# Order of low halves, loads and products in the three pairs of each feed-forward stage

## The reference, cut to what matters

```python
D_MODEL, SEQ, D_FF = 1024, 256, 2816

def swiglu(h, w_in, w_out):                       # first block, stage FFN0
    gate, up = jnp.split(h @ w_in, 2, axis=-1)
    return (jax.nn.silu(gate) * up) @ w_out

def _swiglu(x, wg, wu, wd):                       # stages FFN1 to FFN4
    return (jax.nn.silu(x @ wg) * (x @ wu)) @ wd

def second_block(x, norm_g, ffn_w_gate, ffn_w_up, ffn_w_down, ...):
    for l in range(2):
        g = norm_g[l]
        h = _swiglu(_rmsnorm(x, g[0]), ffn_w_gate[l, 0], ffn_w_up[l, 0], ffn_w_down[l, 0])
        x = x + 0.5 * _rmsnorm(h, g[1])
        h = _rmsnorm(x, g[2])
        h = _mixer_even(h, ...) if l % 2 == 0 else _mixer_odd(h, ...)
        x = x + _rmsnorm(h, g[3])
        h = _swiglu(_rmsnorm(x, g[4]), ffn_w_gate[l, 1], ffn_w_up[l, 1], ffn_w_down[l, 1])
        x = x + 0.5 * _rmsnorm(h, g[5])
    return x
```

## Time and profile before

| | us |
|---|---|
| three runs: median (lowest to highest) | 1301.72 (1301.05 to 1302.33) |
| profiled execution, its time | 1308.35 |
| its span from first to last instruction | 1306.6 |
| PE busy | 1268.1 |
| DVE busy | 970.9 |
| ACT busy | 744.5 |
| POOL busy | 151.7 |

### The profile page before, as it was taken

How to read it: one execution, slowest core, us unless ns; L and a number is a source line. 1 busy time by engine, 2 the same in 40 slices (tenths; PEclk the granted TensorE clock), 3 DMA queues, 4 the chain that set the end, 5 groups by cost and what they waited for, 6 DMA issues and landing times. The chain is left out here.

```text
span 1306.6 us, 17142 instructions
## 1 busy us (share of the span) xinstructions
PE 1268.1 (97%) x6759; PEld 1039.4 (80%) x6759; DVE 970.9 (74%) x989; ACT 744.5 (57%) x922; POOL 151.7 (12%) x132
## 2 busy tenths in 40 slices
PE   8999999999999989999999999999899999999998
PEld 7887888887778868877878777888788897788776
DVE  4476776555898876676797877897776687898865
ACT  4433644444755655657665556565657655755653
POOL 3000197000680000100000000000000100000000
PEclk9999999999999999999999899999999999999989
DMA  9996486555568555652756645956753544668452
GB/s 335 360 401 217 173 283 207 183 184 193 164 235 257 193 145 194 199 173 88 277 192 216 188 150 161 322 198 189 192 177 130 170 143 125 218 232 258 164 149 88
DMA packets 154299, 265.51 MB, mean 203 GB/s; under 512 B 9528, under 2 KB 94836, under 8 KB 152692
## 3 DMA queue, kind: packets, MB, share of 16 engines
q1 hardware_dynamic: 149504, 243.28, 54.8%
q0 software_dynamic: 4352, 21.06, 6.7%
q10 hardware_dynamic: 372, 0.19, 0.1%
HBM read 248.73 MB, written 1.05 MB: 191 GB/s over the span
## 5 line engine op out<-in xcount | busy, mean ns | idle before, releaser
L2151 DVE TENSOR_TENSOR w_lo<-raw,w_hi 128x2048 fp32r<-128x2048 f32 x147 | 340.8, 2324 | 79.4 <-ACT w_hi L1539 79.1
L1539 ACT ACTIVATE w_hi<-raw 128x2048 fp32r<-128x2048 f32 x147 | 280.2, 1911 | 87.8 <-PE ps L763 46.7
L761 PE MATMUL ps<-w_lo,hT_hi 128*128 128x512 f32 x368 | 150.2, 408 | 21.0 <-DVE w_lo L2151 16.4
L762 PE MATMUL ps<-w_hi,hT_hi 128*128 128x512 f32 x368 | 147.6, 401 | 0.0
L763 PE MATMUL ps<-w_hi,hT_lo 128*128 128x512 f32 x368 | 147.1, 400 | 0.0
L761 PE MATMUL ps<-w_lo,xT_pair 128*128 128x512 f32 x308 | 122.4, 397 | 0.0
L763 PE MATMUL ps<-w_hi,xT_pair 128*128 128x512 f32 x308 | 120.2, 390 | 0.0
L762 PE MATMUL ps<-w_hi,xT_pair 128*128 128x512 f32 x308 | 120.0, 390 | 0.0
L761 PE MATMUL ps<-xT_pair,w_hi 128*128 128x256 f32 x368 | 108.3, 294 | 0.2 <-DVE xT_pair L2540 0.2
L761 PEld LDWEIGHTS ps<-w_lo,hT_hi 128*128 128x128 f32 x368 | 71.5, 194 | 42.4 <-issue 19.8
L762 PE MATMUL ps<-xT_pair,w_hi 128*128 128x256 f32 x368 | 104.8, 285 | 0.0
(11 more groups left out here) (335 smaller groups left out, 2663.2 us busy)
## 6 DMA issues: line engine op xcount, KB each, us to landing
raw<-in_ffn_w_down SPq DMA_DIRECT2D x88, 512.0 KB, 4.5
arena<-in_ffn_w_up SPq DMA_DIRECT2D x48, 512.0 KB, 5.4
raw<-in_ffn_w_in SPq DMA_DIRECT2D x44, 512.0 KB, 4.6
raw<-in_ffn_w_gate SPq DMA_DIRECT2D x40, 512.0 KB, 4.1
raw<-in_ffn_w_up SPq DMA_DIRECT2D x40, 512.0 KB, 5.2
raw<-in_conv_w_in SPq DMA_DIRECT2D x24, 512.0 KB, 9.4
arena<-in_ffn_w_gate SPq DMA_DIRECT2D x24, 512.0 KB, 4.6
rows<-in_ffn_w_gate SPq DMA_DIRECT2D x24, 512.0 KB, 6.5
```

The lines of the kernel that those rows point to most:

```text
L761: pe.matmul(o, a_hi, b_lo, start=first, stop=False, skip_group_check=True)
L762: pe.matmul(o, a_hi, b_hi, start=False, stop=False, skip_group_check=True)
L1539: act.activation(w_hi[:, slot_of(n), :], raw[:, raw_slot(n), :], ACT.Copy).then_inc(hi_ready, 1)
L2151: dve.tensor_tensor(w_lo[:, slot_of(n), :], source(n), w_hi[:, slot_of(n), :].bitcast(F32), ALU.subtract).then_inc(raw_done, 1)
```

## The change

It touches only `load_seven`, `row_part` and the three versions of `seven`:

- SP loads down unit 7 ahead of the first pair's blocks and of the wait for `x_new`, and block 3 (b_21) ahead of block 2 (b_22).
- PE's `row_part` takes the eight products with the high weights first, waiting for `hi_ready` alone, and then the four with the low weights, behind `raw_done`. `down` does the like for each tile of tokens: high by high, high by low weights, low hidden by high weights, with a wait ahead of each.
- DVE, first pair: `x_sums_lo` moves ahead of unit 7's low half, `hT_lo` ahead of t_1, unit 8's low half ahead of t_2. Third pair: `hT_lo` and unit 30's low half move ahead of t_1, unit 32's low half ahead of `hT_lo` of down unit 33.

No computation is added or left out.

```diff
--- before.py
+++ after.py
@@ -594,12 +594,12 @@
                 chunk(2, 1)
                 down_rows(4, 0)
                 chunk(5, 2)
+                down_rows(7, 1)
                 sp.wait_ge(x_new, x_count(s - 1, 1, 1))
                 block(0, 0)
                 block(1, 0)
-                down_rows(7, 1)
+                block(3, 0)
                 block(2, 0)
-                block(3, 0)
                 down_rows(12, 2)
                 chunk(16, 5)
                 sp.wait_ge(raw_done, n + 10)
@@ -932,11 +932,16 @@
 
             def row_part(n, h, t, banks):
 
-                hi, lo = unit(n)
+                hi, lo = w_hi[:, slot_of(n), :], w_lo[:, slot_of(n), :]
+                pe.wait_ge(hi_ready, n + 1)
                 for k in range(4):
                     c = slice(k * 512, (k + 1) * 512)
-                    mm = product(ps[:, banks[t], :], xT_hi[:, 4 * h + k, tok(t)], xT_lo[:, 4 * h + k, tok(t)], hi[:, c], lo[:, c],
-                                 h == 0 and k == 0, h == 1 and k == 3)
+                    pe.matmul(ps[:, banks[t], :], xT_hi[:, 4 * h + k, tok(t)], hi[:, c], start=h == 0 and k == 0, stop=False, skip_group_check=True)
+                    pe.matmul(ps[:, banks[t], :], xT_lo[:, 4 * h + k, tok(t)], hi[:, c], start=False, stop=False, skip_group_check=True)
+                pe.wait_ge(raw_done, n + 1)
+                for k in range(4):
+                    mm = pe.matmul(ps[:, banks[t], :], xT_hi[:, 4 * h + k, tok(t)], lo[:, k * 512:(k + 1) * 512], start=False,
+                                   stop=h == 1 and k == 3, skip_group_check=True)
                 return mm
 
             def row_first(n, banks):
@@ -986,9 +991,25 @@
 
                 def down(o, i):
 
-                    pe.wait_ge(hT_ok, NCH * f + i + 1)
+                    hi, lo = w_hi[:, slot_of(n + o), :], w_lo[:, slot_of(n + o), :]
+
+                    def products(t, aT, v, first):
+                        for k in range(2):
+                            for h in range(2):
+                                mm = pe.matmul(ps[:, 4 + 2 * t + h, :], aT[:, k, tok(t)], v[:, k * D + h * 512:k * D + (h + 1) * 512],
+                                               start=first and k == 0, stop=False, skip_group_check=True)
+                        return mm
+
+                    if i == 0:
+                        pe.wait_ge(hT_ok, NCH * f + 1)
+                    pe.wait_ge(hT_hi_ok, NCH * f + i + 1)
+                    pe.wait_ge(hi_ready, n + o + 1)
                     for t in range(TOKT):
-                        mm = down_part(n + o, hT_hi, hT_lo, 0, t, i == 0, False)
+                        products(t, hT_hi, hi, i == 0)
+                        pe.wait_ge(raw_done, n + o + 1)
+                        products(t, hT_hi, lo, False)
+                        pe.wait_ge(hT_ok, NCH * f + i + 1)
+                        mm = products(t, hT_lo, hi, False)
                     mm.then_inc(w_used, 1)
 
                 def pair(p, at, a, b, c, fill):
@@ -2445,12 +2466,12 @@
                 x_sums()
                 row_hidden(1, (2, 3))
                 lo(6)
+                x_sums_lo()
                 lo(7)
-                x_sums_lo()
+                turned(1, 2)
                 sum_first(0)
-                turned(1, 2)
+                lo(8)
                 sum_second(0)
-                lo(8)
                 sum_third(0)
                 row_hidden(2, (0, 1))
                 lo(9, 10, 11)
@@ -2484,13 +2505,13 @@
                 pair_hidden(1, 0)
                 pair_hidden(1, 1)
                 lo(29)
-                sum_first(2)
                 turned(6, 1)
                 lo(30)
+                sum_first(2)
                 sum_second(2)
-                lo(31)
+                lo(31, 32)
                 turned(7, 3)
-                lo(32, 33)
+                lo(33)
                 c_11(2, 2)
                 lo(34, 35, 36)
                 c_22(2)
```

## The result

| | before | after |
|---|---|---|
| timed on one chip, median of 5 runs each (lowest to highest) | 1302.14 (1301.05 to 1304.47) | 1273.71 (1272.33 to 1274.76) |
| ratio, with its 95% interval | | 0.9778 (0.9764 to 0.9792) |
| profiled execution | 1308.35 | 1274.00 |
| its span | 1306.6 | 1272.3 |
| mean granted clock of that execution | 0.989 | 0.998 |

The timed gain is 28.4 us, the forecast was 31.7. The two profiled executions are 34.3 us apart. All three numbers have to be explained.

A forecast was written before the change was run, and what follows sets the result against it. TensorE (PE), busy 97% of the span, was taken as the bound, losing time to waits for low halves and slow clock. Third pair 26.6 plus first pair 5.1 made 31.7 us off 1301.72: 1270.0 us, range 1265 to 1283.

The forecast's parts named there:

- Third pair, both edits: Units 30 to 33 of the four FFN stages: nearly all waiting and slow clock goes, 26.6 us saved in all.
- First pair: Units 7 to 9: unit 7 starts without a wait; 3.5 us saved in FFN1, 0.8 each in FFN2 and FFN3, together 5.1.
- Now the load is issued when unit 4's low half is done: First pair: unit 7's load no longer stands behind two blocks and the wait for x_new; part of the 5.1 us.
- Row units and added waits: Row units' new product order and some 170 more PE waits: value 0, at the upper end 3 us lost.
- the waits hang on the program, not on the profiler, so I take the same 31.7 off: Final sum: the 31.7 us read from the profile also come off the timed median of 1301.72, giving 1270.0.
- The rule weighed in the prediction: Slow clock over 740 to 753, FFN2: rule says 3.4 us lost, against 2.8 in unit 30; it would give 1267.
- K: Rival: PE's clock still falls after the remaining gaps, costing 10.7 us in all, about 1280; chance 0.08.
- D: Rival: DVE becomes the bound, a microsecond or two lost at units 31 and 33 per stage, 1275 to 1278; chance 0.07.
- S: Rival: slower; third pair's accumulating DMA T4 lands late as three megabytes meet, PE waits at unit 36, 1315; chance 0.04.
- N: Rival: no gain; the waits reappear one unit on at full size, 1300; chance 0.03.

## Why the prediction was right, and where it was not

The time, 1273.71, lies in the forecast's own range (1266 to 1276), 3.7 us above its point. The waits and their places were right in the main; the price in time of the slow clock was too high.

- *Third pair, both edits: right.* 27.3 us in the profile, 26.6 forecast. Unit 30's low half followed `hT_lo` by DVE's own lengths as worked out, and t_1, t_2 and the low halves of 31 to 33 kept up. The small waits were 0.28 and 0.28, forecast 0.26 and 0.55. The two edits alone and undone show that both are needed: without DVE's order 13.3 us come back, without the products' 5.0 (by the profiles 15.8 and 6.2).
- *First pair: the sum near, in part by luck.* 5.5 us in the profile, 5.1 forecast, with 1.23 us at unit 9 where 1.5 was forecast. But 1.0 of the 5.5 is FFN3's, a wait that some executions with the old first pair have and others do not; the forecast's 0.8 for it was read off the one that had it. The step "Now the load is issued when unit 4's low half is done" has no share in it: with the loads alone as before nothing changed. And the first pair's edits are worth 4 us only where the products are as before; with the new ones 1.4 (2.4 by the profiles). The step took the edits one by one and forgot that down unit 7 has the new products too.
- *Row units and added waits: right.* 0, by the kernel with the old rows.
- *Short waits: missed.* 1.5 us in the second pairs, at down unit 20; they are gone in each kernel with the new down products and there in each without.
- *The step that failed: "the waits hang on the program, not on the profiler, so I take the same 31.7 off".* The waits do. The slow clock behind them does not: it followed the same wait in two stages of four in one execution and in four of four in another. The profiled execution of before had 0.989 and the most frequent timed run 0.993, and 0.004 x 1300 x 0.84 is 4.4 us. Between profile and time the gain shrank by 5.9: the profile of before lies 6.2 above its median (1308.35 - 1302.14), that of after 0.3 above its own. Of the 5.9 the clock is 4.4, or 5.5 if the run with the median of 1302.14 had 0.994, as the table's 1301.8 suggests. The rest is not explained; the rounding of the clock (0.0005 x 1300 = 0.65 on either side) and the wait of FFN3 may hold it. The 31.7 had the full price of five falls in it: I knew that the profile lay 6.6 above the median and did not ask what of that was clock.
- *The rule weighed in the prediction.* The Trainium skill (TensorE: Matmul & The Clock Gate, Terms) counts the throttled time times one minus the clock's share. The line through the runs has 0.84 of that, and the unit with a window of 0.68 took 1.6 us longer, where (1 - 0.68) x 5.3 says 1.7; over the stretch in which PE partly stands idle it says more than was lost (3.4 for 2.8). So it would have made the forecast worse, by 3 us, as the prediction had it.

The rivals: *K* (the clock still falls) no, the changed kernel's clock fell in none of the four stages. The reason given against it (no fall after 1.10 us) was too weak, as one did come after 1.09 in an experiment. What is left at units 30 and 33 is 0.28, and the 1.23 at unit 9 was not followed by a fall. *D* (DVE the bound at 31 and 33) no: no wait at unit 31. *S* (T4 late) no: it landed after 10.0 us in FFN2, sooner than before, and ACT's copy of unit 36 waited for PE, not for it. Its premise, that three transfers meet, hardly held there. The load beside them was issued between 730 and 731.4 and landed within 4.8 us, and T4 went at 735.06. In the kernel before, the load of 743.5 to 745 took 7.1 and 8.5 us, across T3 and T4. *N* no.

## What to carry to other kernels

Where a product can begin with what comes early, order its terms by when each operand is ready: four to eight matmuls of cover cost nothing and hide 0.9 to 1.8 us of lateness. Two edits that cover the same wait are not worth their sum; price the second with the first already in. Before a gain is read off a profile, compare that execution's granted clock with that of the timed runs, and price waits and slow clock apart. The same goes for a difference of 1 or 2 us between two kernels: compare runs of equal granted clock, or the profiles from a place behind the last stretch that varies.

## What the runs showed of the hardware

- The granted clock does not follow from a wait's length alone. It fell after waits of 1.93 us and not after 2.23 (1.95 and 2.21 in a second kernel), fell after a wait of 1.09 with one of 0.47 ahead of it, and stayed up after two of 2.95. The fall came during the wait or up to 1.4 us after PE had resumed (461.26 with PE's orders alone). What else decides is open; no run here varied it by itself.
- The slow stretches at unit 30 were of two sizes, 3.4 us at 0.50 (0.67 over a window of 5.25) and 6.8 us (0.74 over 13.00). They cost 1.6 and 2.7 us of the unit; part of the longer one fell on the wait.
- A wait that is already satisfied costs PE nothing that shows: with some 170 more of them four matmuls still take 0.91 us, and the kernel without the row units' 64 of them is no faster. The down units' share was not taken out by itself.
- T3 and T4, accumulating DMAs of 1 MB between buffers on the chip, took 7.3 to 8.1 and 10.0 to 11.1 us in the third pairs of the changed kernel, before 8.1 and 11.1 to 12.3.
